# The attention's value weights packed 512 columns wide, two PSUM banks instead of four half-bank pairs

## The reference, cut to what matters

```python
z = h @ w_in[l]
zc = hc @ (w_in[l][:, :COL_Q] if last else w_in[l])
kc = qk_heads(zc[..., COL_K:COL_V])
vc = v_heads(zc[..., COL_V:COL_Q])
...
v = v_heads(z[..., COL_V:COL_Q])
k_all = jnp.concatenate([k, kc], axis=3)
v_all = jnp.concatenate([v, vc], axis=2)
y_a = diff_head_out(diff_attend(q, k_all, v_all, lam), da_subln[l], lam_init)
```

## Time and profile before

| | |
|---|---|
| median of 3 runs | 1914.94 us (1914.7 to 1915.73) |
| the profiled execution, its own time | 1912.17 us |
| its span, first to last instruction | 1910.3 us |
| PE busy | 1878.8 us, 98% of the span |
| DVE busy | 1340.3 us, 70% |
| ACT busy | 1005.2 us, 53% |
| mean granted PE clock | 0.997 |
| moved by DMA | 374.66 MB, mean 196 GB/s |

### The profile page before, as it was taken

How to read it: one execution, slowest core, us unless ns; L and a number is a source line. 1 busy time by engine, 2 the same in 40 slices (tenths; PEclk the granted TensorE clock), 3 DMA queues, 4 the chain that set the end, 5 groups by cost and what they waited for, 6 DMA issues and landing times.

```text
span 1910.3 us, 26445 instructions
## 1 busy us (share of the span) xinstructions
PE 1878.8 (98%) x10784; PEld 1595.7 (84%) x10784; DVE 1340.3 (70%) x1834; ACT 1005.2 (53%) x1459; POOL 37.9 (2%) x45
## 2 busy tenths in 40 slices
PE   6999999999999999999899999999999999999998
PEld 3899888999888998988788887788888888778886
DVE  5688789888789888865665566765566555786555
ACT  4365545565545655544544456554456444666444
POOL 1300000000000000000000000000000000000000
PEclk9999999999999999999999999999999999999999
DMA  9645676545676643465477754367765777536775
GB/s 362 217 145 180 224 242 199 182 131 176 221 242 198 210 152 128 163 209 188 132 214 226 231 187 149 129 203 229 224 196 183 228 224 223 173 111 197 225 228 165
DMA packets 123144, 374.66 MB, mean 196 GB/s; under 512 B 14032, under 2 KB 32592, under 8 KB 122256
## 3 DMA queue, kind: packets, MB, share of 16 engines
q1 hardware_dynamic: 118320, 352.11, 57.2%
q0 software_dynamic: 4416, 19.37, 3.0%
q10 hardware_dynamic: 288, 1.51, 0.2%
HBM read 360.34 MB, written 10.49 MB: 194 GB/s over the span
## 4 chain that ended last, share of the span: by engine, by line
PE 92%; DVE 4%; ACT 2%; DMA 1%; issue 1%; SPq 0%; DVEq 0%; ACTq 0%
PE PS L657 28%; PE PS L659 27%; PE PS L658 27%; DVE w_lo L2079 2%; PE PS L844 1%; PE PS L863 1%; DMA raw<-weights 1%; ACT w_hi L1502 1%; PE PS L954 1%; PE PS L1106 1%; PE PS L1237 1%; PE PS L935 1%; PE PS L1226 1%; PE PS L853 0%; PE PS L753 0%
## 5 line engine op out<-in xcount | busy, mean ns | idle before, releaser
L2079 DVE TENSOR_TENSOR w_lo<-raw,w_hi 128x1024 fp32r<-128x1024 f32 x600 | 730.8, 1232 | 391.7 <-ACT w_hi L1502 390.5
L1502 ACT ACTIVATE w_hi<-raw 128x1024 fp32r<-128x1024 f32 x600 | 625.4, 1056 | 446.3 <-DMA raw<-weights 443.1
L657 PE MATMUL PS<-w_hi,h_hi 128*128 128x512 f32 (+1 forms) x1248 | 481.7, 386 | 1.3 <-DVE w_lo L2079 1.3
L659 PE MATMUL PS<-w_hi,h_lo 128*128 128x512 f32 (+1 forms) x1248 | 475.8, 381 | 0.0
L658 PE MATMUL PS<-w_lo,h_hi 128*128 128x512 f32 (+1 forms) x1248 | 475.7, 381 | 0.0
L657 PEld LDWEIGHTS PS<-w_hi,h_hi 128*128 128x128 f32 x1248 | 234.7, 188 | 52.4 <-issue 4.5
L657 PE MATMUL PS<-h_hi,w_hi 128*128 128x256 f32 x928 | 270.0, 291 | 3.4 <-DVE h_lo L2097 2.7
L659 PEld LDWEIGHTS PS<-w_hi,h_lo 128*128 128x128 f32 x1248 | 234.7, 188 | 45.6
L658 PEld LDWEIGHTS PS<-w_lo,h_hi 128*128 128x128 f32 x1248 | 234.8, 188 | 44.3 <-issue 1.0
L658 PE MATMUL PS<-h_lo,w_hi 128*128 128x256 f32 x928 | 263.0, 283 | 0.0
L659 PE MATMUL PS<-h_hi,w_lo 128*128 128x256 f32 x928 | 262.9, 283 | 0.0
(11 more groups left out here) (293 smaller groups left out, 1711.9 us busy)
## 6 DMA issues: line engine op xcount, KB each, us to landing
raw<-weights SPq DMA_DIRECT2D x610, 512.0 KB, 3.7
act_mem<-arena SPq DMA_DIRECT2D x144, 64.0 KB, 3.1
arena<-act_mem SPq DMA_DIRECT2D x36, 256.0 KB, 3.6
qk<-weights POOLq DMA_DIRECT2D x12, 512.0 KB, 5.1
v<-weights POOLq DMA_DIRECT2D x12, 512.0 KB, 4.1
x<-weights SPq DMA_DIRECT2D x8, 512.0 KB, 7.9
qk<-cond_in POOLq DMA_DIRECT2D x2, 1024.0 KB, 5.1
arena<-arena SPq DMA_DIRECT2D x32, 64.0 KB, 2.7
```

What stands on the lines that cost most here:

```text
L657: pe.matmul(dst, hi, m_hi_, start=first, stop=False, **kw)
L659: return pe.matmul(dst, lo, m_hi_, start=False, stop=last, **kw)
L1502: nc.scalar.activation(w_hi[:, r, :], raw[:, r, :], ACT.Copy).then_inc(w_hi_ready, 1)
L2079: V.tensor_tensor(w_lo[:, r, :], raw[:, r, :], f32(w_hi[:, r, :]), ALU.subtract).then_inc(w_lo_ready, 1)
```

## The change

The value columns of `w_in` are packed differently: a slot now holds 256 rows of the contraction for all 512 columns, instead of 512 rows for 256 columns. Size and number of the slots are the same. `token_pair` goes. `value_slots` does two slots at a time with 512-wide matmuls, one bank per token tile, and all four slots accumulate into the same two banks, 0 and 1. In its first half it goes over the two slots once for each token tile, with the wait for bank 1 (`taken(p, 3)`) between the two, so a slot is counted as used in the second half of that. Neither bank is finished before the fourth slot. So both copies on DVE now stand in round 1 of `run_pass`: bank 0 waits for a new counter, `v_half`, which goes up after the last matmul of token tile 0, and bank 1 for the fourth slot. The context's values of layer 1 go the same way, and ACT copies both banks at the end.

```diff
-            def token_pair(c, bank, hi=h_hi, lo=h_lo, tiles=None, between=None):
-                for half in range(2):
-                    slot_ready(c + half)
-                    r = (c + half) % RING
...
-                            mm = mm3(PS[:, bank, t * T:(t + 1) * T], hi[:, kk, tok], lo[:, kk, tok], w_hi[:, r, w], w_lo[:, r, w],
-                                     kk == 0 and t == 0, kk == KD - 1, skip_group_check=True)
-                            if between is not None and (half, t, j) == (0, 0, 1):
-                                between()
+            def value_slots(p, first):
+
+                c = start[f"pass{p}"] + part["v"]
+                if first:
                     for t in range(TT):
+                        for j in range(2):
+                            if t == 0:
+                                slot_ready(c + j)
+                            mm = wide(c + j, j, t, t, h_hi, h_lo)
+                            if t == 1:
+                                mm.then_inc(w_used, 1)
+                        if t == 0:
+                            pe.wait_ge(*taken(p, 3))
+                    return
+                for j in (2, 3):
+                    slot_ready(c + j)
+                    for t in range(TT):
+                        mm = wide(c + j, j, t, t, h_hi, h_lo)
+                        if (j, t) == (3, 0):
+                            mm.then_inc(v_half, 1)
                     mm.then_inc(w_used, 1)
...
                 pe.wait_ge(*taken(p, 2))
-                token_pair(c0 + part["v"], 0)
+                value_slots(p, True)
...
-                    pe.wait_ge(*taken(p, j - 2))
                     if j == 5:
-                        token_pair(c0 + part["v"] + 2, 1)
+                        value_slots(p, False)
                     else:
+                        pe.wait_ge(*taken(p, j - 2))
                         project(c0 + 2 * j, PS[:, j % 2, 0:T])
...
-            def ctx_values(j, between=None):
-                pe.wait_ge(src_ready, 4 * OUT_EVENT[1] + 3 + j)
-                token_pair(start["ctx_v"] + 2 * j, 4 + j, g_hi, g_lo, between=between)
+            def ctx_values(first, between=None):
+                pe.wait_ge(src_ready, 4 * OUT_EVENT[1] + 4)
+                for j in (first, first + 1):
+                    c = start["ctx_v"] + j
+                    slot_ready(c)
+                    for t in range(TT):
+                        mm = wide(c, j, t, 4 + t, g_hi, g_lo)
+                        if (j, t) == (first, 0) and between is not None:
+                            between()
+                    mm.then_inc(w_used, 1)
...
-            def take_ctx_values(j):
-                act.wait_ge(w_used, start["ctx_v"] + 2 * j + 2)
...
+            def take_ctx_values():
+                act.wait_ge(w_used, start["ctx_v"] + 4)
+                for t in range(TT):
+                    nc.scalar.activation(v[:, 2 + t, :], PS[:, 4 + t, :], ACT.Copy).then_inc(ctx_taken, 1)
...
-                take_values(c0 + part["v"], 0, v[:, kt:kt + 2, 0:T], dve_evac)
...
                 for n in range(8):
+                    if n == 1:
+                        if p == 0:
+                            dve.wait_ge(spec_pair, 1)
+                        take_values(p, 0)
                     if n >= 1 or ON_CTX[p]:
                         softmax_max(p, n)
 
                     if n == 1:
-                        take_values(c0 + part["v"] + 2, 1, v[:, kt:kt + 2, T:2 * T], dve_evac)
+                        take_values(p, 1)
...
-        token(w, 512, 1024)
+        wide(w[:, 512:1024])
```

More of the change, by code:

```diff
@@ L381, in build @@
         dve_evac = sem("dve_evac")
+        v_half = sem("v_half")
         ctx_taken = sem("ctx_taken")
@@ L1450, in _ @@
             norm_groups(5)
-            ctx_values(1, lambda: norm_total(5))
+            ctx_values(2, lambda: norm_total(5))
             filter_columns(1, 3)
@@ L1541, in take_ctx_keys @@
                                      ACT.Copy).then_inc(ctx_taken, 1)
-            def take_ctx_values(j):
-                act.wait_ge(w_used, start["ctx_v"] + 2 * j + 2)
-                nc.scalar.activation(v[:, 2:4, j * T:(j + 1) * T], PS[:, 4 + j, :].rearrange("p (t c) -> p t c", t=TT),
-                                     ACT.Copy).then_inc(ctx_taken, 1)
+            def take_ctx_values():
+                act.wait_ge(w_used, start["ctx_v"] + 4)
+                for t in range(TT):
+                    nc.scalar.activation(v[:, 2 + t, :], PS[:, 4 + t, :], ACT.Copy).then_inc(ctx_taken, 1)
             def between_passes():
@@ L1565, in between_passes @@
                 split(c + 5 + AHEAD)
-                take_ctx_values(0)
                 copy_groups(5)
@@ L1571, in between_passes @@
                     high(3, lambda kk: mod[:, 1, kk, 0:1], h_hi, *BEHIND_SUMS[j])
-                take_ctx_values(1)
+                take_ctx_values()
                 split(c + 7 + AHEAD)
@@ L2240, in ada_row, with take_values @@
                                            accum_out=ada_sums[:, i:i + 1]).then_inc(ada_sum, 1)
-            def take_values(c, bank, dst, done):
-                dve.wait_ge(w_used, c + 2)
-                V.tensor_copy(dst, PS[:, bank, :].rearrange("p (t c) -> p t c", t=TT)).then_inc(done, 1)
+            def take_values(p, t):
+                if t == 0:
+                    dve.wait_ge(v_half, p + 1)
+                else:
+                    dve.wait_ge(w_used, start[f"pass{p}"] + part["v"] + 4)
+                V.tensor_copy(v[:, (2 if ON_CTX[p] else 0) + t, :], PS[:, t, :]).then_inc(dve_evac, 1)
             def softmax_max(p, n):
@@ L2325, in keys_queries @@
                         behind(j)
-                kt = 0 if on_x else 2
                 split(c0 + part["v"] + AHEAD)
@@ L2329, in keys_queries @@
                     softmax_max(p, 0)
-                if p == 0:
-                    dve.wait_ge(spec_pair, 1)
-                take_values(c0 + part["v"], 0, v[:, kt:kt + 2, 0:T], dve_evac)
                 if on_x:
@@ L2339, in run_pass @@
                 c0 = start[f"pass{p}"]
-                kt = 0 if not ON_CTX[p] else 2
                 for n in range(8):
+                    if n == 1:
+                        if p == 0:
+                            dve.wait_ge(spec_pair, 1)
+                        take_values(p, 0)
                     if n >= 1 or ON_CTX[p]:
```

## The result

The changed kernel took 1921.57 us (median of 22 runs, 1915.32 to 1925.24) beside 1916.2 us for the kernel before (22 runs, 1912.0 to 1918.24). The ratio is 1.0026, 95% interval 1.0020 to 1.0032: slower by 0.26% (the two medians alone give 1.0028). The forecast, 1919.4 us on 1914.94 us, was a ratio of 1.0023. The profiled execution took 1921.84 us, with a span of 1920.0 us and a mean granted clock of 0.990.

The account below looks back on a forecast made before the run. PE's chain, 92% of the page, was taken as the bound. Losses 2.6 + 0.3 + 0.2 + 0.2 = 3.3 us, the 2.9 us saving included, plus 1.2 for the clock: 4.5 us, 1919.4 us on 1914.94; range 1915.5 to 1921.2.

Parts of the forecast that it names:

- Step 1: Value matmuls on PE: 48 wide at 0.227 us replace 96 narrow in each of four places, 0.73 us saved each.
- Step 2: First hyena projection: PE idles for DVE's late value copy, some 3 us in pass 0, some 1 in passes 1 and 2.
- The mix: DVE in pass 0: without the copy between low parts, the mix ends at 93.5 in place of 94.41, 0.9 us earlier.
- Step 3: Pass 0 loads: SP issues slot 13 about 1.2 us later, and ACT waits for the DMA of slot 14.
- the other end of the range: Pass 0 if slot 14 were not late: only two splits and the copy follow the mix, 0.9 us lost.
- The forecast for pass 0: First hyena projection starts at 98.3 in place of 95.67: 2.6 us lost, behind a PE wait of 3.3 us.
- Pass 1: First hyena projection starts at 374.05 in place of 373.76: 0.3 us lost; ends 1.2 lost or 0.7 won.
- context's values: Layer 1's context values: PE wins 0.7 us, but pass 2's third projection waits; 0.2 lost, ends 0.7 won and 0.6 lost.
- step 4: Pass 2's third projection: again released by a low part, which waits for ACT behind two copies, 0.5 to 0.6 us more.
- Pass 2: First hyena projection: same order on all engines as pass 1, not worked out further; 0.2 us taken as lost.
- Step 5: Behind pass 0's wait: granted clock near 0.5 for some microseconds, taken as 1.2 us lost.
- the bound I had: Upper end of the clock's cost behind pass 0's wait: 1.5 us, from 16 narrow matmuls slowed in an earlier stretch.

Follow-up runs that it names:

- all_mended: Changed kernel with bank 0's copy right behind the mix, first half slot by slot, ACT's split ahead of the two context copies: 1914.8 us, ratio 0.9993.
- pool_later: Changed kernel with one edit, POOL's second batch of filter sums waiting until slot 15 is free: 1919.48 us, ratio 1.0026.

## Why the prediction was right, and where its steps were off

**Step 1, the pace.** The mechanism held; the size was 0.56 us in a place, not 0.73. In pass 1 the values took 11.62 us before and 11.06 to 11.08 in the changed kernel and its nine variants; in pass 0 the halves gave 0.28 and 0.27 where nothing waited. (The table's 0.51 for pass 1 holds 0.05 us of drift ahead of it.) That is 0.012 us for each of 48 matmuls saved, where I had 0.015. My 0.121 was the mean of a whole group and my 0.2267 the pace inside one; but the first step of a group takes longer, 0.22 us narrow and 0.34 wide, and this 0.1 us more is paid once whatever the width. The four places are worth about 2.1 us where nothing waits, and gave 1.8 in the changed kernel. By the gap that the Trainium skill gives for an isolated matmul ("TensorE: Matmul & The Clock Gate", "Back-to-back issue gap") it would have been an estimated 0.5; here the trace decides.

**Step 2, the copy of bank 0 behind two splits.** Right, and shown twice: with the copy moved forward the wait went, and with the copy moved back in the kernel before it came.

**The mix, part of step 2.** This failed. I had it end at 93.5, 0.9 us earlier, because the copy no longer stood between the low parts of slots 11 and 12. It ended where it had been. The two rows carried the sign of it: 2.56 and 2.44 us for what is 1.2 us in the pair of the last row. I read them as the price of these instructions and never asked what made them twice as long. It was POOL's work beside them, and its end sets the end of the low part. In the Trainium skill, "SBUF — State Buffer", section "Terms", DVE and GpSimd are said to lock one shared pair of ports for a whole instruction, so that the loser is fully blocked. The trace agrees: counted from the start of the values, POOL's sums ended at 5.01 and 8.38 us and the two low parts at 6.09 and 9.46, each 1.08 us behind a sum, about the 1.2 us that a low part takes alone. Without POOL's batch the pair is 3.57 us shorter.

**Step 3, slot 14.** The chain was right link by link. `layer` was issued 1.23 us later from the start of the values (forecast 1.2). Slot 14 landed 7.0 us after its issue, 1.0 us later than before (forecast 1.2). The projection came 2.3 us later (forecast 2.6). What was wrong was the other end of the range: I had 0.9 us lost if slot 14 were in time, and the experiments gave 1.8, since the mix had not moved. The forecast for pass 0 came out nearly right because I took the end at which the mix does not count.

**Pass 1** gave +0.33 us (0.3), the **context's values** +0.25 (0.2), with the releaser named in step 4; `all_mended` shows that ACT's order was its cause. **Pass 2** missed in sign: -0.55 in place of +0.2. There DVE's copy (from 693.66 us, 0.68 long) ended 0.08 us before the projection that needs it, so nothing was waited for. I had taken pass 1's order for it without reading its transfers. With `layer` moved to behind slot 16 pass 2 has a wait of 0.36 us, in `pool_later` one of 0.83 us, so it stands on that edge. Why it stands on the good side in the changed kernel was not tested.

**Step 5, the clock.** Right in kind, too small: 2.63 us lost, not 1.2. I took the length of one stretch from before, 3.4 us, as the most there could be; this one was 6.8. The waits of 1.80 and of 3.15 us had 3.4 us behind them, with 1.3 to 1.5 us lost, the bound I had. Up to the last microseconds of the program every such stretch of the kernel before is 3.4 us long, so its trace did not show the longer one. What decides between the two lengths, and whether the clock falls at all, stays open: the wait of 5.02 us went with either length, and the wait of 2.81 us with no fall.

In sum, 0.3 too much for pass 0, 0.75 too much for pass 2 and 1.4 too little for the clock made 4.5 in place of 4.96 us. That the total came so near is partly luck, of errors that cancel and of a profile in which the clock fell for the longer time.

## What to carry to other kernels

When wider tiles finish two buffers at the end instead of one in the middle, price the drain first: here, in one pair of profiles, the waits and the clock behind them cost 6.8 us where the wider matmuls saved 1.8. Put the drain ahead of work that is needed later, and then look for the second chain that ends just behind it, because two nearly equal chains hide each other from any single edit. When equal instructions have different durations in one trace, find out what runs beside the long ones before you shift them.

## What the hardware showed that I had not expected

Two DVE subtractions of 128x1024 took 5.93 us beside POOL's two sums and 2.36 us without them, and POOL's second sum itself took 3.41 us there and 2.45 us when moved away. And behind a stall of 2.38 us on PE the clock's fall cost more than the stall itself, 2.63 us, while in another kernel a stall of 2.81 us at the same place cost nothing beyond itself in the profiled execution.
